# The first sub-layer's opening by quarters instead of halves, with joined shift and scale steps and fewer condition products on TensorE

## The chip, the core and the metric

The kernel runs on one core of a Trainium2 chip. TensorE multiplies, VectorE, ScalarE and GpSimd do element-wise work, SyncE issues most DMAs. The metric is the device time of one execution in microseconds; before, it is 1519.99 us (median of 3 runs, 1519.05 to 1521.19).

## What is computed

Two layers, each a half-step SwiGLU network, a hybrid token mixer and a second half-step SwiGLU network, on 256 tokens of 1024 features in float32. The change touches only what stands ahead of the first network: the normalised input is scaled and shifted by two rows that come from the condition vector c through the matrix w_ada.

```python
mod = jax.nn.silu(c) @ w_ada[i] + b_ada[i]
sh1, sc1, g1, sh2, sc2, g2, sh3, sc3, g3 = jnp.split(mod, 3 * N_SUBLAYERS, axis=-1)
h = modulate(rms_norm(x, norm_pre[i, 0]), sh1, sc1)      # h * (1 + scale) + shift
y = swiglu_ffn(h, w_ffn_in[i, 0], w_ffn_out[i, 0])
x = x + 0.5 * g1[:, None, :] * rms_norm(y, norm_post[i, 0])
```

## The kernel before

There are six sub-layers (s = 0 to 5). Each streams its weights in chunks of 512 KB. SyncE loads a chunk into one of eight `w_raw` slots, ScalarE rounds it into `w_hi` (line 1213), VectorE computes the remainder `w_lo` = `w_raw` - `w_hi` (line 1522), and TensorE multiplies. For each weight tile it makes three products: `w_hi` with `h_hi` (717), `w_lo` with `h_hi` (718), `w_hi` with `h_lo` (710). A chunk of the first network's input matrix is twelve such products of 512 columns. Each engine runs its own list in program order; semaphores join the lists, and an instruction that waits holds up all behind it on its engine.

A chunk of the input matrix is a pair (u, q): unit u (0 to 10) is 512 output columns (256 gate, 256 up), q (0 to 3) is one quarter of the 1024 rows, so it needs one quarter of the features of h. Sub-layer 0 takes its chunks in `FIRST_ORDER`: units 0 to 2 with q = 0 and 1 (chunks 0 to 5), then units 0 to 2 with q = 2 and 3 (chunks 6 to 11), then unit by unit. When a unit has its four chunks, ScalarE takes silu of the gate part, VectorE multiplies (`act_by_token`, 1722), TensorE turns the result (`act_turn`, 752); chunk 12 is the first of unit 3, ahead of which `act_turn(1)` stands.

To have h at all, sub-layer 0 needs the scale row (part 1 of `ada_acc`) and the shift row (part 0), each the sum of 8 slabs of w_ada (128 rows each, times one element of silu(c) per partition) and a bias, and then a sum over the 128 partitions. One slab step on VectorE is a `scalar_tensor_tensor` that adds slab times c to the accumulator (`first_steps`, 1550); each waits for the step before it. The first half (512 features) of the scale row is made wholly on TensorE (862, 866), two of eight slabs of the shift's first half too (883); the other 22 half-steps run on VectorE. Then VectorE scales x by the row (1561, 1571), TensorE multiplies by the diagonal of the root mean square (`rstd_diagonal`) which also turns the tile (894), and adds the shift in the same bank (901); ScalarE rounds to `h_hi` (1285), VectorE takes `h_lo` (1581). This is done in two halves: the second stands between chunks 3 and 5 on TensorE.

Of the kernel before, what the change touches and what calls it, by code (L numbers as in the profile page):

```python
# [11 lines left out]
ALU = mybir.AluOpType  # L12
AX_X = mybir.AxisListType.X

P = 128
# [59 lines left out]
FIRST_ORDER = [(u, q) for u in range(EARLY) for q in (0, 1)] + [(u, q) for u in range(EARLY) for q in (2, 3)]  # L75
# [192 lines left out]
def build(nc, x_d, c_d, w_ada, b_ada, norm_pre, norm_post, w_ffn_in, w_ffn_out, w_in, pool_w, w_ret_out, w_pool_out,  # L268
          w_ssm_out, w_fox_out, w_out, vecs_d, consts_d, out_d):
    with ExitStack() as ctx:  # L270
# [49 lines left out]
        DG, dg_off = sb("rstd_diagonal", [P, TT, P])  # L320
# [104 lines left out]
        first_a_ps = sem("first_half_scale_row_in_psum")  # L425
        first_pre = [sem(f"first_pre_row_landed{s}") for s in range(2)]
        late_x = sem("second_half_x_scaled")
# [128 lines left out]
        def _(sp):  # L556
# [50 lines left out]
            def pre_row(t):  # L607
                if t == 1:
                    sp.wait_ge(late_x, 2)
# [12 lines left out]
            def first_slabs(n, half, pair):  # L622

                ks = slice(2 * pair * P, (2 * pair + 2) * P)
                col = PARTS[n] * D + half * HALF
                sp.dma_start(PSLAB[:, 8 * n + 2 * pair:8 * n + 2 * pair + 2, half * HALF:(half + 1) * HALF],
                             w_ada[0, ks, col:col + HALF].rearrange("(k p) n -> p k n", p=P))\
                    .then_inc(ada_first[8 * n + 4 * half + pair], 16)
# [8 lines left out]
            first_slabs(0, 0, 0)  # L637
            for order, n in enumerate(PARTS):
                bias(0, n, order)
            for pair in range(1, 4):  # L640
                first_slabs(0, 0, pair)
            sp.dma_start(KC[:, 0:P], consts_d[:, 0:P]).then_inc(ident_landed, 16)
            first_row(0)
            for pair in range(4):
                first_slabs(1, 0, pair)
            for g in range(3):
                chunk(g)
            first_slabs(0, 1, 0)
            first_slabs(0, 1, 1)
            chunk(3)  # L650
            first_slabs(0, 1, 2)
            first_slabs(0, 1, 3)
            first_row(1)
            first_slabs(1, 1, 0)
            first_slabs(1, 1, 1)
            chunk(4)
            first_slabs(1, 1, 2)
            first_slabs(1, 1, 3)
            for g in range(5, N_RAW):
                chunk(g)  # L660
# [3 lines left out]
            for s in range(SUBS):  # L664
                l = s // 3
                for c in range(COUNT[s]):
# [3 lines left out]
                    if s + 1 < SUBS and c == 3:  # L670
# [21 lines left out]
        def _(pe):  # L692
# [10 lines left out]
            def token_chunk(g, j, banks, hi, lo, kn, tts, lo_ready=None):  # L703

                wh, wl = weights(g)
                parts = [(kk, tt) for kk in range(2) for tt in tts]
# [20 lines left out]
            def ffn_in(s, c):  # L727
# [7 lines left out]
                if s == 0 and c == 0:  # L735
                    pe.wait_ge(hh_ok.sem, hh_ok.at(0, 2))

                    def ready():
                        pe.wait_ge(hl_ok.sem, hl_ok.at(0, 2))
                if s == 0 and c == 2 * EARLY:  # L740
                    pe.wait_ge(hl_ok.sem, hl_ok.at(0, 4))
# [117 lines left out]
            def first_scale_row():  # L859

                pe.wait_ge(bias_landed[1].sem, bias_landed[1].at(0, 16))
                mm(PS[:, 4, :], ones, part(1)[:, 0:HALF], start=True, stop=False)
                for k in range(KD):
                    if k % 2 == 0:
                        pe.wait_ge(ada_first[k // 2], 16)
                    ins = mm(PS[:, 4, :], CS[:, k:k + 1].to_broadcast([P, P]), PSLAB[:, k, 0:HALF], start=False,  # L866
                             stop=(k == KD - 1))
                ins.then_inc(first_a_ps, 1)

            def late_scale_row():  # L870

                pe.wait_ge(first_used, FIRST_SCALE)
                pe.wait_ge(hl_ok.sem, hl_ok.at(0, 2))
                mm(PS[:, 6, :], ones, part(1)[:, HALF:D], start=True, stop=True).then_inc(a_ps.sem, 1)

            def first_pair_of_shifts():

                pe.wait_ge(ada_first[8], 16)
                pe.wait_ge(xsq_ok.sem, xsq_ok.at(0, 4))
                for tt in range(TT):  # L880
                    for k in range(4):
                        for i in range(2):
                            mm(PS[:, 6 + tt, k * P:(k + 1) * P], PSLAB[:, 8 + i, k * P:(k + 1) * P],
                               CS[:, i:i + 1].to_broadcast([P, P]), start=(k == 0 and i == 0), stop=False)

            def first_turn(half, tt):

                if half == 0:
                    pe.wait_ge(f_ok.sem, scaled(0, tt + 1))
                else:  # L890
                    pe.wait_ge(late_x, tt + 1)
                for k in range(4):
                    cs = slice(half * HALF + k * P, half * HALF + (k + 1) * P)
                    mm(PS[:, 6 + tt, k * P:(k + 1) * P], Y[:, tt, cs], DG[:, tt, :], start=(half == 1 and k == 0), stop=False)

            def first_shifts(half, tt):

                pe.wait_ge(first_used, FIRST_SHIFT if half == 0 else LATE_SHIFT)
                for k in range(4):
                    cs = slice(half * HALF + k * P, half * HALF + (k + 1) * P)  # L900
                    ins = mm(PS[:, 6 + tt, k * P:(k + 1) * P], part(0)[:, cs], ones, start=False, stop=(k == 3))
                ins.then_inc(t_ps.sem, 1)
# [10 lines left out]
            def ffn(s):  # L913
# [272 lines left out]
            first_scale_row()  # L1186
            first_pair_of_shifts()
            for tt in range(TT):
                first_turn(0, tt)
            for tt in range(TT):  # L1190
                first_shifts(0, tt)
# [8 lines left out]
        def _(act):  # L1200
# [80 lines left out]
            def first_h_hi(half):  # L1281

                for tt in range(TT):
                    act.wait_ge(t_ps.sem, t_ps.at(0, 2 * half + tt + 1))
                    fn(HH[:, 4 * half:4 * half + 4, tt * P:(tt + 1) * P], PS[:, 6 + tt, :].rearrange("p (k t) -> p k t", k=4),
                       ACT.Copy).then_inc(hh_ok.sem, 1)
# [35 lines left out]
            def ffn(s):  # L1322
                f = 2 * (s // 3) + (s % 3) // 2
                for c in range(N_FFN - TAIL):
# [13 lines left out]
                    if s == 0 and c == 1:  # L1338
                        split_to(6)
                        first_h_hi(1)  # L1340
# [14 lines left out]
            def mixer(s):  # L1355
                layer = s // 3
                n_gate, n_sz, n_xbc = 0, 0, 0
                for c in range(N_MIX - TAIL):
# [62 lines left out]
                    if c == 1 and layer == 0:  # L1421
                        fn(SEL[0:32, :], ident[0:32, 0:20], ACT.Copy)
                        fn(SEL[32:64, :], ident[32:64, 32:52], ACT.Copy)
# [74 lines left out]
            split_to(0)  # L1498
            first_h_hi(0)
            split_to(4)  # L1500
# [8 lines left out]
        def _(dve):  # L1509
# [31 lines left out]
            def first_steps(a, b):  # L1541

                for m in range(a, b):
                    n, half, k = FIRST_STEPS[m]
                    cs = slice(half * HALF, (half + 1) * HALF)
                    dve.wait_ge(ada_first[8 * n + 4 * half + k // 2], 16)
                    dve.wait_ge(bias_landed[PARTS[n]].sem, bias_landed[PARTS[n]].at(0, 16))
                    if m:
                        dve.wait_ge(first_used, m)
                    dve.scalar_tensor_tensor(part(PARTS[n])[:, cs], PSLAB[:, 8 * n + k, cs], CS[:, k:k + 1],  # L1550
                                             part(PARTS[n])[:, cs], ALU.mult, ALU.add).then_inc(first_used, 1)

# [624 lines left out]
```

## Time and profile before

| | before |
|---|---|
| median of 3 runs | 1519.99 us |
| profiled execution, its time | 1519.76 us |
| profiled execution, its span | 1517.7 us |
| TensorE busy | 1487.8 us, 98% |
| VectorE busy | 1134.8 us, 75% |
| ScalarE busy | 778.9 us, 51% |
| DMA, mean over the span | 226 GB/s |

The span runs from the first to the last instruction that the profile holds; the time of the same execution is 2.1 us more. TensorE is busy nearly all the time, so the question for an edit at the start is when it gets into that state, and how much of its work is done by then.

### The profile page before, as it was taken

To read this page: it belongs to the slowest core of one execution; us is meant where nothing else is said; L and a number is where in the kernel's file an instruction comes from. 1 tells how busy PE (TensorE), PEld (TensorE's weight loads), DVE (VectorE), ACT (ScalarE), POOL (GpSimd) and SP (SyncE) were. 2 spreads that over 40 slices of the span, in tenths; PEclk is the share of its full clock that TensorE was granted. 3 is DMA by queue.
4 is the path that set the end of the run, shared out by engine and by line. 5 is a ranking of instruction groups with operands and counts; after the bars stand their busy time and mean duration, and the time that the engine had idled before them with its cause. 6 is when DMAs were issued, how large, how long until landed. Compare 5 with 4: busy or idle time off the path is not lost.

```text
span 1517.7 us, 20003 instructions
## 1 busy us (share of the span) xinstructions
PE 1487.8 (98%) x7776; PEld 1260.4 (83%) x7776; DVE 1134.8 (75%) x1339; ACT 778.9 (51%) x970; POOL 165.5 (11%) x96
## 2 busy tenths in 40 slices
PE   7999999999999999999999999999999999999998
PEld 4788888998978887888878888799988888878886
DVE  5887767867899888677686777767878988774453
ACT  3444455556473556454464444654746545654443
POOL 0000002303411110000000000040324011000000
PEclk9999999999999999999999999999999999999999
DMA  9899866656677856888768887565567787556652
GB/s 355 285 305 298 310 217 210 174 151 190 201 245 248 276 182 221 258 275 274 239 200 258 279 268 252 174 192 158 167 199 230 239 266 243 175 181 185 187 188 97
DMA packets 199778, 343.42 MB, mean 226 GB/s; under 512 B 18546, under 2 KB 109938, under 8 KB 199684
## 3 DMA queue, kind: packets, MB, share of 16 engines
q1 hardware_dynamic: 181540, 276.08, 57.9%
q10 hardware_dynamic: 18144, 66.07, 13.1%
q8 instruction: 61, 1.00, 0.3%
q14 instruction: 33, 0.27, 0.1%
HBM read 341.05 MB, written 1.05 MB: 225 GB/s over the span
## 4 chain that ended last, share of the span: by engine, by line
PE 87%; DVE 9%; issue 2%; ACT 2%; DMA 0%; SPq 0%; ACTq 0%; DVEq 0%
PE ps L717 16%; PE ps L710 16%; PE ps L718 16%; PE ps L794 6%; PE ps L795 6%; PE ps L796 6%; PE ps L1151 4%; PE ps L1153 4%; PE ps L1152 4%; DVE w_lo L1522 2%; DVE ada_acc L1538 1%; PE ps L752 1%; DVE ada_acc L1550 1%; PE ps L835 1%; PE ps L866 1%
## 5 line engine op out<-in xcount | busy, mean ns | idle before, releaser
L1522 DVE TENSOR_TENSOR w_lo<-w_raw,w_hi 128x1024 fp32r<-128x1024 f32 x480 | 611.4, 1296 | 110.6 <-ACT w_hi L1213 110.2
L1213 ACT ACTIVATE w_hi<-w_raw 128x1024 fp32r<-128x1024 f32 x490 | 507.6, 1053 | 353.7 <-DMA w_raw<-in_w_ffn_in 121.2
L717 PE MATMUL ps<-w_hi,h_hi 128*128 128x512 f32 x1026 | 407.4, 397 | 4.6 <-DVE w_lo L1522 3.1
L718 PE MATMUL ps<-w_lo,h_hi 128*128 128x512 f32 x1026 | 400.5, 390 | 0.0
L710 PE MATMUL ps<-w_hi,h_lo 128*128 128x512 f32 x1026 | 398.0, 391 | 0.0
L717 PEld LDWEIGHTS ps<-w_hi,h_hi 128*128 128x128 f32 x1026 | 193.0, 188 | 47.9 <-DVE w_lo L1522 6.5
L710 PEld LDWEIGHTS ps<-w_hi,h_lo 128*128 128x128 f32 x1026 | 192.7, 188 | 42.2 <-DVE h_lo L1678 1.0
L718 PEld LDWEIGHTS ps<-w_lo,h_hi 128*128 128x128 f32 x1026 | 193.3, 188 | 38.3
L1538 DVE SCALAR_TENSOR_TENSOR ada_acc<-ada_slab,c_silu,ada_acc 128x1024 f32<-128x1024 f32 x128 | 187.0, 1461 | 14.1 <-DMA ada_slab<-in_w_ada 14.1
L1151 PE MATMUL ps<-h_hi,w_hi 128*128 128x256 f32 x640 | 183.0, 286 | 0.0
L1153 PE MATMUL ps<-h_hi,w_lo 128*128 128x256 f32 x640 | 181.0, 283 | 0.0
L1152 PE MATMUL ps<-h_lo,w_hi 128*128 128x256 f32 x640 | 181.0, 283 | 0.0
L794 PE MATMUL ps<-w_hi,act_hi 128*128 128x512 f32 x352 | 137.6, 391 | 0.0
L795 PE MATMUL ps<-w_lo,act_hi 128*128 128x512 f32 x352 | 137.0, 389 | 0.0
L796 PE MATMUL ps<-w_hi,act_lo 128*128 128x512 f32 x352 | 137.0, 389 | 0.0
L1722 DVE TENSOR_TENSOR act_by_token<-gate_silu,ps 128x512 f32<-128x512 f32 x44 | 30.2, 687 | 131.5 <-PE ps L710 118.0
L1151 PEld LDWEIGHTS ps<-h_hi,w_hi 128*128 128x128 f32 x640 | 122.7, 192 | 1.2 <-issue 0.3
L1152 PEld LDWEIGHTS ps<-h_lo,w_hi 128*128 128x128 f32 x640 | 122.8, 192 | 0.2
L1153 PEld LDWEIGHTS ps<-h_hi,w_lo 128*128 128x128 f32 x640 | 122.7, 192 | 0.0
L2038 POOL MEMSET ada_acc<- 128x1024 f32 x18 | 17.0, 953 | 644.6 <-PE ps L847 597.5
L1333 ACT ACTIVATE gate_silu<-ps 128x512 f32<-128x512 f32 x44 | 26.3, 597 | 111.9 <-PE ps L710 111.3
L796 PEld LDWEIGHTS ps<-w_hi,act_lo 128*128 128x128 f32 x352 | 66.1, 188 | 13.9
(286 smaller groups left out, 1666.8 us busy)
## 6 DMA issues: line engine op xcount, KB each, us to landing
w_raw<-in_w_ffn_in SPq DMA_DIRECT2D x352, 256.0 KB, 3.6
w_raw<-in_w_in SPq DMA_DIRECT2D x168, 512.0 KB, 3.7
ada_slab<-in_w_ada ACTq DMA_DIRECT2D x126, 512.0 KB, 4.7
w_raw<-in_w_ffn_out SPq DMA_DIRECT2D x88, 512.0 KB, 4.4
ada_slab_first<-in_w_ada SPq DMA_DIRECT2D x16, 512.0 KB, 8.8
w_raw<-in_w_ssm_out SPq DMA_DIRECT2D x16, 512.0 KB, 4.4
w_raw<-in_w_out SPq DMA_DIRECT2D x16, 512.0 KB, 3.4
w_raw<-in_w_pool_out SPq DMA_DIRECT2D x8, 512.0 KB, 3.7
```

The source lines that it names most:

```text
L710: return mm(PS[:, banks + tt, :], lo[:, k, tok(tt)], wh[:, kk * HALF:(kk + 1) * HALF], start=False, stop=(k == kn - 1))
L717: mm(out, hi[:, k, tok(tt)], wh[:, cs], start=(k == 0), stop=False)
L718: mm(out, hi[:, k, tok(tt)], wl[:, cs], start=False, stop=False)
L794: mm(out, hi[:, k, tok(tt)], wh[:, cs], start=first, stop=False)
L795: mm(out, hi[:, k, tok(tt)], wl[:, cs], start=False, stop=False)
L796: return mm(out, lo[:, k, tok(tt)], wh[:, cs], start=False, stop=last)
L1151: mm(out, wh[:, cs], HH[:, k, :], start=(k == 0 and t % 2 == 0), stop=False)
L1152: mm(out, wh[:, cs], HL[:, k, :], start=False, stop=False)
L1153: ins = mm(out, wl[:, cs], HH[:, k, :], start=False, stop=(k == KD - 1 and t % 2 == 1))
L1213: fn(WH[:, n % N_HI, 0:width], RAW[:, n % N_RAW, 0:width], ACT.Copy).then_inc(w_hi, 1)
L1522: dve.tensor_tensor(WL[:, n % N_RAW, 0:width], RAW[:, n % N_RAW, 0:width], WH[:, n % N_HI, 0:width], ALU.subtract).then_inc(w_lo, 1)
L1538: dve.scalar_tensor_tensor(part(n), slab, CS[:, k:k + 1], part(n), ALU.mult, ALU.add)\
```

## The change

Chunks 0 to 11 are taken quarter by quarter: units 0 to 2 with q = 0, then 1, 2, 3. The slabs are loaded by quarters (256 columns, four slabs of one part per DMA, still 16 DMAs of 512 KB). One VectorE step now takes a slab's quarter of the shift and of the scale together (128 x 2 x 256). For the first quarter four of the eight slabs (0, 1, 4, 5) are products on TensorE, both parts in one product; for the other quarters all eight are VectorE steps. TensorE's product with ones sums both rows at once, once a quarter. The diagonal is gone: VectorE applies the root and the shift itself (`first_h_full`), and TensorE turns the result (`pe.transpose`, 4 per quarter). Other edits: for the first chunk of every quarter the products with `h_hi` and `w_hi` come first, then those with `w_lo`, then those with `h_lo`; ScalarE's silu table is loaded ahead of the first chunk; and the second sub-layer's row of norm_pre is asked for later.

```diff
-FIRST_ORDER = [(u, q) for u in range(EARLY) for q in (0, 1)] + [(u, q) for u in range(EARLY) for q in (2, 3)]
+QUARTER = D // 4
+FIRST_ORDER = [(u, q) for q in range(4) for u in range(EARLY)]
 FIRST_ORDER += [(u, q) for u in range(EARLY, UNITS) for q in range(4)]
...
-FIRST_STEPS = [(1, 0, k) for k in range(2, 8)] + [(0, 1, k) for k in range(8)] + [(1, 1, k) for k in range(ADA_FIRST)]
-FIRST_SHIFT, FIRST_SCALE, LATE_SHIFT = 6, 14, 22
+def on_pe(q):
+
+    return () if q else (0, 1, 4, 5)
+
+
+FIRST_STEPS = [(q, k) for q in range(4) for k in range(8) if k not in on_pe(q)]
...
+            def first_rows_of(q):
+
+                out = PS[:, 7, :].rearrange("p (n c) -> p n c", n=2)
+                slabs = PSLAB[:].rearrange("p (n k) c -> p n k c", n=2)
+                for i, k in enumerate(on_pe(q)):
+                    for n in range(2):
+                        pe.wait_ge(ada_first[4 * q + 2 * n + k // 4], 16)
+                    mm(out, CS[:, k:k + 1].to_broadcast([P, P]), slabs[:, :, k, q * QUARTER:(q + 1) * QUARTER], start=(i == 0),
+                       stop=False)
+                pe.wait_ge(first_used, first_steps_of(q)[1])
+                mm(out, ones, ACC[:, 0:2 * D].rearrange("p (n c) -> p n c", n=2)[:, :, q * QUARTER:(q + 1) * QUARTER],
+                   start=(not on_pe(q)), stop=True).then_inc(first_rows if q < 3 else a_ps.sem, 1)
+
+            def first_turn(q):
+
                 for tt in range(TT):
...
+                    for k in range(2):
+                        ins = pe.transpose(PS[:, 6, k * T + tt * P:k * T + (tt + 1) * P],
+                                           Y[:, tt, (2 * q + k) * P:(2 * q + k + 1) * P], ident)
                 ins.then_inc(t_ps.sem, 1)
...
-                    if s == 0 and c == 3:
-                        late_scale_row()
-                    if s == 0 and c in (4, 5):
-                        for tt in range(TT):
-                            (first_turn if c == 4 else first_shifts)(1, tt)
+                    if s == 0 and c in (2, 5, 8):
+                        first_rows_of(c // 3 + 1)
+                    if s == 0 and c in (3, 6, 9):
+                        first_turn(c // 3)
...
+            fn(DUMMY[:], one, ACT.Silu)
+            for q in range(4):
+                split_to(3 * q)
+                first_h_hi(q)
...
+            for q in range(4):
+                split_to(3 * q)
+                first_h_lo(q)
+                if q == 3:
+                    break
+                split_to(3 * q + 1)
+                first_steps(q + 1)
+                split_to(3 * q + 2)
...
+                first_x_scale(q + 1)
+                first_h_full(q + 1)
```

VectorE, from the first `h_lo` to the x scaling of the second half, before; `first_steps` is line 1550 and `split_to` line 1522:

```order
L1581 TENSOR_TENSOR h_lo<-ps,h_hi 128x4x128 x2
L1522 TENSOR_TENSOR w_lo<-w_raw,w_hi 128x1024
L1550 SCALAR_TENSOR_TENSOR ada_acc<-ada_slab_first,c_silu,ada_acc 128x512 x4
L1522 TENSOR_TENSOR w_lo<-w_raw,w_hi 128x1024
L1550 SCALAR_TENSOR_TENSOR ada_acc<-ada_slab_first,c_silu,ada_acc 128x512 x4
L1522 TENSOR_TENSOR w_lo<-w_raw,w_hi 128x1024
L1561 SCALAR_TENSOR_TENSOR scale_row<-ps,scale_row 128x512
L1571 TENSOR_TENSOR y_tok<-x_res,scale_row 128x512 x2
```

Now, from one quarter's `h_lo` (1576) to the next quarter's, with the steps in line 1545, the remainders in line 1512, the x scaling in 1563 and the root and shift in 1570; this block stands three times in a row:

```order
L1576 TENSOR_TENSOR h_lo<-ps,h_hi 128x512
L1512 TENSOR_TENSOR w_lo<-w_raw,w_hi 128x1024
L1545 SCALAR_TENSOR_TENSOR ada_acc<-ada_slab_first,c_silu,ada_acc 128x2x256 x8
L1512 TENSOR_TENSOR w_lo<-w_raw,w_hi 128x1024
L1556 SCALAR_TENSOR_TENSOR scale_row<-ps,scale_row 128x256
L1563 TENSOR_TENSOR y_tok<-x_res,scale_row 128x256 x2
L1570 SCALAR_TENSOR_TENSOR y_tok<-y_tok,small_columns,ps 128x256 x2
L1512 TENSOR_TENSOR w_lo<-w_raw,w_hi 128x1024
```

Eight steps in a row now stand ahead of each row sum, and three chunks' remainders are spread between them.

VectorE at the end of the opening, before, from the last `h_lo` (1581) to the product of the first finished unit (1722; 1538 is a slab step of the gate row):

```order
L1581 TENSOR_TENSOR h_lo<-ps,h_hi 128x4x128 x2
L1522 TENSOR_TENSOR w_lo<-w_raw,w_hi 128x1024 x6
L1722 TENSOR_TENSOR act_by_token<-gate_silu,ps 128x512
L1522 TENSOR_TENSOR w_lo<-w_raw,w_hi 128x1024
L1538 SCALAR_TENSOR_TENSOR ada_acc<-ada_slab,c_silu,ada_acc 128x1024
```

And now (1712 is that product, 1528 that slab step):

```order
L1576 TENSOR_TENSOR h_lo<-ps,h_hi 128x512
L1512 TENSOR_TENSOR w_lo<-w_raw,w_hi 128x1024 x3
L1528 SCALAR_TENSOR_TENSOR ada_acc<-ada_slab,c_silu,ada_acc 128x1024
L1512 TENSOR_TENSOR w_lo<-w_raw,w_hi 128x1024
L1528 SCALAR_TENSOR_TENSOR ada_acc<-ada_slab,c_silu,ada_acc 128x1024
L1712 TENSOR_TENSOR act_by_token<-gate_silu,ps 128x512
```

The first finished unit's product moved behind two slab steps; the last `h_lo` comes before chunk 9 and not before chunk 6.

## Rows read from the trace of the kernel before

**Rows 1.** Page, part 1: busy us, share of the span, instructions.
```profile
PE 1487.8 (98%) x7776; PEld 1260.4 (83%) x7776; DVE 1134.8 (75%) x1339; ACT 778.9 (51%) x970; POOL 165.5 (11%) x96
```

**Rows 2.** Stretches: busy time of each engine, PEclk (granted clock), DMA share, GB/s.
```profile
10.00:50.00 40.00, 35.02 (x167) 25.00 (x166) 29.14 (x42) 8.86 (x12) 0.95 (x1) 1.00 1.06 388
...
50.00:200.00 150.00, 150.00 (x687) 123.93 (x687) 119.87 (x115) 73.73 (x84) 3.81 (x4) 1.00 0.88 293
```

**Rows 3.** Waits of TensorE from 50 us on: us in total, times, longest.
```profile
PE ps L835 <- DVE y_tok L1669: 7.9, 5, 1.6
```

**Rows 4.** Chain of waits, 0 to 52 us, shares by line.
```profile
by line: DVE ada_acc L1550 28.9%; PE ps L866 16.5%; issue 12.2%; DMA ada_acc<-in_b_ada 10.4%; PE ps L901 7.9%; PE ps L862 3.9%; DVE y_tok L1571 2.7%; DVE scale_row L1561 2.7%; PE ps L874 2.2%; SPq L636 1.9%; ACT w_hi L1213 1.8%; DVEq L1549 
```

**Rows 5.** Timeline of VectorE: start us, us, what, idle before.
```profile
17.22 1.65 DVE L1550 SCALAR_TENSOR_TENSOR ada_acc<-ada_slab_first,c_silu,ada_acc 128x512 f32<-128x512 f32 x2 [5.90 <-DMA ada_slab_first<-in_w_ada]
...
34.12 3.40 DVE L1550 SCALAR_TENSOR_TENSOR ada_acc<-ada_slab_first,c_silu,ada_acc 128x512 f32<-128x512 f32 x4
...
37.44 1.22 DVE L1522 TENSOR_TENSOR w_lo<-w_raw,w_hi 128x1024 fp32r<-128x1024 f32 x1
...
39.22 0.69 DVE L1561 SCALAR_TENSOR_TENSOR scale_row<-ps,scale_row 128x512 f32<-128x512 f32 x1 [0.57 <-PE ps L874]
...
50.89 0.69 DVE L1581 TENSOR_TENSOR h_lo<-ps,h_hi 128x512 fp32r<-128x512 f32 x1 [0.51 <-ACT h_hi L1285]
...
52.39 6.89 DVE L1522 TENSOR_TENSOR w_lo<-w_raw,w_hi 128x1024 fp32r<-128x1024 f32 x6
...
61.95 1.28 DVE L1538 SCALAR_TENSOR_TENSOR ada_acc<-ada_slab,c_silu,ada_acc 128x1024 f32<-128x1024 f32 x1
```

**Rows 6.** Groups of VectorE by form, whole span: count, busy us, mean ns.
```profile
L1550 DVE SCALAR_TENSOR_TENSOR ada_acc<-ada_slab_first,c_silu,ada_acc 128x512 f32<-128x512 f32 x22 | 16.5, 750 | 8.0 <-DMA ada_slab_first<-in_w_ada 5.9
...
L1911 DVE SCALAR_TENSOR_TENSOR xbc<-xbc,vectors,ps 128x256 f32<-128x256 f32 x16 | 6.9, 471 | 0.0
```

**Rows 7.** Timeline of TensorE's products.
```profile
10.17 8.79 PE L866 MATMUL ps<-ada_slab_first,c_silu 128*128 128x512 f32 x16
...
27.60 0.50 PE L717 MATMUL ps<-w_hi,h_hi 128*128 128x512 f32 x1 [0.69 <-ACT h_hi L1285]
...
37.58 1.12 PE L874 MATMUL ps<-ada_acc,small_columns 128*128 128x512 f32 x2 [0.29 <-DVE ada_acc L1550]
...
45.75 0.50 PE L717 MATMUL ps<-w_hi,h_hi 128*128 128x512 f32 x1 [2.22 <-DVE w_lo L1522]
...
67.95 0.60 PE L752 MATMUL ps<-consts,act_by_token 128*128 128x128 f32 x4
...
68.31 0.48 PE L717 MATMUL ps<-w_hi,h_hi 128*128 128x512 f32 x1
...
71.16 0.39 PE L717 MATMUL ps<-w_hi,h_hi 128*128 128x512 f32 x1
```

**Rows 8.** Timeline of TensorE's weight loads.
```profile
8.30 0.50 PEld L862 LDWEIGHTS ps<-ada_acc,small_columns 128*128 128x128 f32 x2 [8.30 <-issue]
...
12.74 0.34 PEld L866 LDWEIGHTS ps<-ada_slab_first,c_silu 128*128 128x128 f32 x1 [0.52 <-issue]
...
14.08 0.19 PEld L866 LDWEIGHTS ps<-ada_slab_first,c_silu 128*128 128x128 f32 x1 [0.24 <-issue]
```

**Rows 9.** Timeline of ScalarE.
```profile
26.95 0.60 ACT L1285 ACTIVATE h_hi<-ps 128x512 fp32r<-128x512 f32 x1 [0.30 <-PE ps L901]
...
27.44 2.95 ACT L1213 ACTIVATE w_hi<-w_raw 128x1024 fp32r<-128x1024 f32 x3
```

**Rows 10.** Timeline of SyncE's queue: the first slabs.
```profile
2.32 0.43 SPq L626 DMA_DIRECT2D ada_slab_first<-in_w_ada  x1
...
3.96 1.48 SPq L626 DMA_DIRECT2D ada_slab_first<-in_w_ada  x3
```

**Rows 11.** DMA issues, 2.3 to 2.7 us: KB, us to landing.
```profile
ada_slab_first<-in_w_ada SPq DMA_DIRECT2D x1, 512.0 KB, 5.7
```

**Rows 12.** DMA issues, 4.9 to 5.3 us: KB, us to landing.
```profile
ada_slab_first<-in_w_ada SPq DMA_DIRECT2D x1, 512.0 KB, 7.4
```

More of the change, by code:

```diff
@@ L243, in __call__, with first_steps_of @@
         self.need(self.mark(ins))
-FIRST_STEPS = [(1, 0, k) for k in range(2, 8)] + [(0, 1, k) for k in range(8)] + [(1, 1, k) for k in range(ADA_FIRST)]
-FIRST_SHIFT, FIRST_SCALE, LATE_SHIFT = 6, 14, 22
+def on_pe(q):
+    return () if q else (0, 1, 4, 5)
+FIRST_STEPS = [(q, k) for q in range(4) for k in range(8) if k not in on_pe(q)]
+def first_steps_of(q):
+    m = [i for i, step in enumerate(FIRST_STEPS) if step[0] == q]
+    return m[0], m[-1] + 1
 def vector_table(b_forget, pool_scale, conv_w, conv_b, dt_bias, a_log, d_skip, ssm_norm):
@@ L636, in _ @@
                 sp.dma_start(X[:, tt, :], x_d[0, tt * P:(tt + 1) * P, :]).then_inc(x_landed[tt], 16)
-            first_slabs(0, 0, 0)
+            first_slabs(0, 0)
             for order, n in enumerate(PARTS):
                 bias(0, n, order)
-            for pair in range(1, 4):
-                first_slabs(0, 0, pair)
+            first_slabs(0, 1)
+            first_row(0)
             sp.dma_start(KC[:, 0:P], consts_d[:, 0:P]).then_inc(ident_landed, 16)
[L643 to L659, printed above, removed]
+            for q in range(4):
+                if q:
+                    first_slabs(q, 0)
+                    first_slabs(q, 1)
+                    if q == 2:
+                        first_row(1)
+                chunk(2 * q)
+                chunk(2 * q + 1)
+            for g in range(8, N_RAW):
                 chunk(g)
@@ L669, in _ @@
                     chunk(BASE[s] + c + N_RAW)
-                    if s + 1 < SUBS and c == 3:
+                    if s + 1 < SUBS and c == (3 if s else 10):
                         pre_row(s + 1)
@@ L703, in token_chunk @@
             def token_chunk(g, j, banks, hi, lo, kn, tts, lo_ready=None):
+                parts = [(kk, tt) for kk in range(2) for tt in tts]
+                if g < 3 * EARLY + 1 and lo_ready is not None:
+                    pe.wait_ge(w_hi, g + 1)
+                    wh = WH[:, g % N_HI, :]
+                    for kk, tt in parts:
+                        mm(PS[:, banks + tt, :], hi[:, 2 * j + kk, tok(tt)], wh[:, kk * HALF:(kk + 1) * HALF],
+                           start=(2 * j + kk == 0), stop=False)
+                    _, wl = weights(g)
+                    for kk, tt in parts:
+                        mm(PS[:, banks + tt, :], hi[:, 2 * j + kk, tok(tt)], wl[:, kk * HALF:(kk + 1) * HALF], start=False,
+                           stop=False)
+                    lo_ready()
+                    for kk, tt in parts:
+                        k = 2 * j + kk
+                        ins = mm(PS[:, banks + tt, :], lo[:, k, tok(tt)], wh[:, kk * HALF:(kk + 1) * HALF], start=False,
+                                 stop=(k == kn - 1))
+                    return ins
                 wh, wl = weights(g)
-                parts = [(kk, tt) for kk in range(2) for tt in tts]
                 def lo_product(kk, tt):
@@ L857, in shift_sums @@
                 column_sums(0, t, bank).then_inc(sh_ps.sem, 1)
[L859 to L879, printed above, removed]
-                for tt in range(TT):
[L881 to L901, printed above, removed]
+            def first_rows_of(q):
+                out = PS[:, 7, :].rearrange("p (n c) -> p n c", n=2)
+                slabs = PSLAB[:].rearrange("p (n k) c -> p n k c", n=2)
+                for i, k in enumerate(on_pe(q)):
+                    for n in range(2):
+                        pe.wait_ge(ada_first[4 * q + 2 * n + k // 4], 16)
+                    mm(out, CS[:, k:k + 1].to_broadcast([P, P]), slabs[:, :, k, q * QUARTER:(q + 1) * QUARTER], start=(i == 0),
+                       stop=False)
+                pe.wait_ge(first_used, first_steps_of(q)[1])
+                mm(out, ones, ACC[:, 0:2 * D].rearrange("p (n c) -> p n c", n=2)[:, :, q * QUARTER:(q + 1) * QUARTER],
+                   start=(not on_pe(q)), stop=True).then_inc(first_rows if q < 3 else a_ps.sem, 1)
@@ L1185, in _ @@
             pe.wait_ge(c_ok, 1)
[L1186 to L1191, printed above, removed]
+            first_rows_of(0)
+            pe.wait_ge(xsq_ok.sem, xsq_ok.at(0, 4))
+            pe.wait_ge(ident_landed, 16)
+            first_turn(0)
             for s in range(SUBS):
@@ L1279, in h_hi, with first_h_hi @@
                        PS[:, 2 * tt + half, :].rearrange("p (k t) -> p k t", k=4), ACT.Copy).then_inc(hh_ok.sem, 1)
[L1281 to L1286, printed above, removed]
+            def first_h_hi(q):
+                act.wait_ge(t_ps.sem, t_ps.at(0, q + 1))
+                fn(HH[:, 2 * q:2 * q + 2, :], PS[:, 6, :].rearrange("p (k t) -> p k t", k=2), ACT.Copy).then_inc(hh_ok.sem, 1)
             def boundary(s):
```

129 lines of the change are left out of this document (55 added, 74 removed).

## The prediction, made before the changed kernel ran

> **What bounds the kernel now.** I read the page first: TensorE is busy 98% of the span [rows 1], so an edit pays or costs only through the time at which TensorE gets its work. The stretches say where that is open: from 50 to 200 us TensorE is busy in all of 150 us, from 10 to 50 us in 35.0 of 40, and much of that is not network work but the making of the rows [rows 2]. After 50 us the largest wait is 7.9 us at the five later boundaries, which the change leaves alone [rows 3]. So the whole effect is this: at what time does TensorE start chunk 12 (by then chunks 0 to 11 and two `act_turn` are done in both kernels)? Before, that is 71.16 us [rows 7]. What is behind it is paced by TensorE.
>
> Inside the opening the chain of waits puts 28.9% on VectorE's slab steps, more than on any other line, and 16.5% on the first rows' products on TensorE [rows 4]. The timeline of VectorE shows the steps in packs of four, a remainder `w_lo` between them, with no idle time ahead of the packs [rows 5]; TensorE waits for VectorE ahead of chunk 4 for 2.22 us [rows 7]. The DMA share is full (1.06, 388 GB/s) [rows 2], but VectorE waits for a slab once only, ahead of the first pack [rows 5]. So VectorE paces the opening once the first slabs are in.
>
> **Unit costs.** A pack of four steps takes 3.40 and one is 0.75 long, so a dependent step comes every (3.40 - 0.75) / 3 = 0.88 us [rows 5, 6]. `w_lo` is 1.22 long, six take 6.89, one each 1.13 [rows 5]. The gate row's step is 1.28, about 1.20 apart [rows 5]. ScalarE rounds a chunk in 1.06 (three in 2.95) and an `h_hi` tile in 0.60, 0.50 apart [rows 9]. A row sum on TensorE is 1.12 [rows 7]; a turn of four tiles lands in 0.60 and holds TensorE for 0.36 (67.95 to 68.31) [rows 7]; chunk 11 takes 2.85 (68.31 to 71.16), of which the turn's tail is about 0.1, so a chunk alone is 2.72 to 2.75 [rows 7]; I use 2.72 and 0.1 behind a turn. The joined step (128 x 2 x 256) is in no row. The nearest is the 512-column step, same elements, 0.75; from below it is bounded by 0.47, the 256-column form of the operation, from above by two of those, 0.94 [rows 6]. With the 0.13 of the wait: 0.60 to 1.07, and I take 0.88, since both ends would need cost to go by rows and not by elements. The 256-column scaling and shifting operations: 0.47 each [rows 6], five in 2.1 with their overlaps.
>
> **The first quarter.** The first slab lands at 2.3 + 5.7 = 8.0, the fourth at 4.95 + 7.4 = 12.35 (its issue is the third one's of the three from 3.96) [rows 10 to 12]; at 388 GB/s the second is 1.35 behind the first, 9.4. Here four slab DMAs are the whole quarter. VectorE: two steps from 9.5, two from 12.4, end 14.05, then the five small operations of the second root to 15.2. TensorE: products at 9.4 and 11.1 at the slow pace (weight loads 0.34 long, 0.52 between, 1.7 per product; 0.19 and 0.24 later, 0.86 per product [rows 8]), then two more with the quicker pace coming in between, then the sum: 16.5, with 15.7 if the quick pace comes at once at 12.8, and 17.4 if only at the end. Then 2.1 for VectorE's five (18.7), the turn and `h_hi` (19.8). Chunks 0 and 1 are 0.33 MB (row and identity) and 1.05 MB behind the fourth slab, 3.6 us at 388 GB/s, so in by 16, ahead of their use. TensorE starts chunk 0 at 19.8 where it did at 27.60 [rows 7]: 7.8 us earlier. Behind `h_hi` ScalarE rounds chunk 1 (20.8), VectorE takes its remainder, and the second quarter's first step starts at 21.95.
>
> **The cycle of a quarter.** From there, in order: eight steps 7 x 0.88 + 0.75 = 6.9; the remainder of chunk 3q+2, 1.22 (TensorE's row sum, 1.12, lies beside it at no cost; without that cover it would add 1.1); 0.1 for semaphores; chunk 3q+2 on TensorE, 2.72, because `first_turn` stands behind it; the turn 0.6; `h_hi` 0.50 until ScalarE is free; then ScalarE's rounding of chunk 3q+4, 1.06, which stands behind `h_hi`, and its remainder on VectorE, 1.13; 0.1. Sum 14.4. VectorE's scaling and shift (2.1), one remainder and `h_lo` lie beside chunk 3q+2 and the turn: work of 2.1 + 1.2 against 3.3, so they cost nothing, but also hide nothing more. Data isn't late: the slabs of the second quarter are 3.5 MB behind the first quarter's last, 9 us at 388 GB/s, so 21.4, just ahead of the first step, and a later quarter needs 3.7 MB in 14.4 us. Over three cycles, `h_hi` of the fourth quarter starts at 21.95 + 2 x 14.4 + 11.7 = 62.4 (11.7 is the cycle up to there).
>
> **The end of the opening.** Chunk 9 starts at 63.1, chunk 10 ends at 68.5. But chunk 11 stands behind `act_turn(0)`, and VectorE reaches that unit's product only after: rounding of chunk 10 on ScalarE (64.0), three remainders 3.4, step 1.2, remainder 1.13, step 1.2, product 0.7: 71.65. TensorE waits 3.2 us there, turns, chunk 11 from 72.1, turn, chunk 12 at 75.1. Against 71.16 that is 3.9 us later. The balance in another way: VectorE does 28 steps instead of 22 (6 x 0.88 = 5.3 us more), and none of TensorE's freed time can be used.
>
> **The sum.** 1519.76 (profiled execution) + 3.9 = 1523.7. The median of the runs is 0.2 above that execution, so 1523.9; I say 1524.0. A difference under 0.2%, 3.0 us, can't be told from none.
>
> **A rival by the clock of TensorE.** The granted clock reads 1.00 in all stretches [rows 2], and yet the same weight load takes 0.34 early and 0.19 from 14 us [rows 8], as if between 1.2 and 2.4 GHz, after TensorE had been busy for 5 us. The new opening has TensorE idle three times for 3.4 us (chunk 3q+1 ends 3.4 ahead of the row sum), and 3.2 before `act_turn(0)`. The longest pause before was 2.22, and the product behind it took the usual 0.50, as at 27.60 [rows 7]; no row shows a longer one here. If the pace falls, a row sum costs 1.8 instead of 1.1 and chunk 3q+2 up to 1.6 more; both are in the cycle: 2 us each quarter, 6 us in all, 1530.
>
> The Trainium skill ("TensorE: Matmul & The Clock Gate", Part 1, the HAM clock gate) says that an idle TensorE falls back to 1.2 GHz, which speaks against this change; by that rule the sum would be the 1530 of this rival, by the row of the 2.22 us pause 1524.
>
> **Other rivals.** The joined step is cheap: if it goes at the pace of its 256-element rows, 0.60, each quarter is 2 us shorter: 3.9 - 6.0, 1518; it needs 0.55 or less to win over 0.2%. For it: the opening's chain is these steps. Against it: 22 rows of the 512-column form at 0.75, and 0.47 for half of that, a cost by elements [rows 6]. This is the case on the other side. A plainer form of it, that the 7.8 us gained at chunk 0 simply stay, would give 1512; it needs VectorE's cycle to be TensorE's (three chunks, sum, turn: 9.7 us), and the eight steps alone are 6.9 of that with three remainders behind them; I give it nothing of its own.
>
> The loss is real but small: the quick pace comes early (15.7, -0.8) and semaphores and the idle tenths that I add come to less; 1520 to 1523, not to be told from no change. For it: my terms hold 0.1 to 0.3 us per quarter of such waits.
>
> **Chances.** Forecast mechanism with over 3.0 us lost: 0.58. Clock falls: 0.10. Same mechanism but under 3.0 us, 0.22, and a step somewhat cheaper, 0.03. Cheap step that wins: 0.07. So faster 0.07, same 0.25, slower 0.68. The likeliest case alone spans 1523 to 1526 (first rows at 15.7 to 17.4, waits). The range has to reach the clock's 1530 above and the small loss below: 1519.5 to 1530.
>
> **What would show it.** Right: first product of chunk 0 near 19.8; joined steps 0.75 long; first steps of the quarters 14.4 apart; TensorE idle about 3.4 us ahead of each row sum and about 3 us ahead of the first `act_turn`; chunk 12 at 75. Wrong: joined steps near 0.5 or 0.9, VectorE idle on slabs, products of chunk 2, 5, 8 at twice their length, or TensorE busy throughout from 45 us on.

## The result and the profile after

The changed kernel takes 1531.93 us (median of 4 runs, 1529.38 to 1533.34), the kernel before 1520.59 us on the same chip (4 runs, 1519.05 to 1522.37). The ratio is 1.0071, with a 95% interval of 1.0059 to 1.0084: slower by 0.7%, or 11.3 us. The forecast was 1524.0 with a range up to 1530, so the sign was right and the loss nearly three times as large as said. The profiled execution took 1531.35 us with a span of 1529.5.

First the page of after, its part 1 (busy time, share of the span, instructions), which answers to [rows 1]:

```profile
PE 1485.6 (97%) x7692; PEld 1255.1 (82%) x7692; DVE 1143.8 (75%) x1357; ACT 778.5 (51%) x971; POOL 165.5 (11%) x96
```

TensorE has 84 products fewer and 2.2 us less of busy time, and the span is 11.8 us longer. So the time is not lost with more work; it goes to TensorE being idle, or to the same products taking longer. The stretches of after tell where (columns as in [rows 2]: busy time of PE, PEld, DVE, ACT, POOL, then the granted clock, DMA share, GB/s):

```profile
20.00:40.00 20.00, 15.41 (x59) 11.43 (x60) 16.07 (x23) 6.10 (x7) 0.00 (x0) 0.91 1.09 383
40.00:60.00 20.00, 13.78 (x51) 9.75 (x49) 15.70 (x22) 4.50 (x5) 0.00 (x0) 0.91 0.82 287
60.00:82.00 22.00, 17.33 (x58) 12.93 (x59) 17.63 (x21) 8.43 (x10) 1.90 (x2) 0.77 0.48 160
82.00:200.00 118.00, 118.00 (x540) 97.52 (x539) 97.09 (x93) 57.24 (x65) 2.87 (x3) 1.00 0.90 299
```

TensorE is idle for 4.6, 6.2 and 4.7 us in the three stretches from 20 us on, and the granted clock, 1.00 in both rows of [rows 2], is 0.91, 0.91 and 0.77. From 82 to 200 us it is never idle and the clock reads 1.00. The DMA share is full up to 40 us and falls after that, and none of the waits below is for a DMA.

The waits of TensorE from 19 to 83 us (us in total, times, longest) name what it waits for; the two largest:

```profile
PE ps L885 <- DVE ada_acc L1545: 10.0, 3, 3.3
PE ps L768 <- DVE act_by_token L1712: 2.9, 1, 2.9
```

The last joined step of a quarter holds up the row sum (885) three times for 3.3 us, and the first unit's product (1712) holds up `act_turn` (768) once for 2.9. The chain of events is plainest in TensorE's timeline of after, which answers to [rows 7] (start, us, what, idle before):

```profile
9.55 6.73 PE L882 MATMUL ps<-ada_slab_first,c_silu 128*128 128x512 f32 x8 [9.55 <-DMA ada_slab_first<-in_w_ada]
...
20.59 1.20 PE L712 MATMUL ps<-w_hi,h_hi 128*128 128x512 f32 x4 [0.69 <-ACT h_hi L1277]
...
29.65 2.08 PE L885 MATMUL ps<-ada_acc,small_columns 128*128 128x512 f32 x2 [3.31 <-DVE ada_acc L1545]
30.79 1.37 PE L735 MATMUL ps<-w_hi,h_hi 128*128 128x512 f32 x1
31.95 0.63 PE L736 MATMUL ps<-w_lo,h_hi 128*128 128x512 f32 x1
...
34.85 0.60 PE L896 MATMUL ps<-consts,y_tok 128*128 128x128 f32 x4
36.13 1.19 PE L712 MATMUL ps<-w_hi,h_hi 128*128 128x512 f32 x4 [0.69 <-ACT h_hi L1277]
...
45.19 1.12 PE L885 MATMUL ps<-ada_acc,small_columns 128*128 128x512 f32 x2 [3.32 <-DVE ada_acc L1545]
46.33 0.72 PE L735 MATMUL ps<-w_hi,h_hi 128*128 128x512 f32 x1
...
50.08 0.39 PE L735 MATMUL ps<-w_hi,h_hi 128*128 128x512 f32 x1
...
50.77 0.60 PE L896 MATMUL ps<-consts,y_tok 128*128 128x128 f32 x4
52.06 1.19 PE L712 MATMUL ps<-w_hi,h_hi 128*128 128x512 f32 x4 [0.69 <-ACT h_hi L1277]
...
61.12 2.07 PE L885 MATMUL ps<-ada_acc,small_columns 128*128 128x512 f32 x2 [3.32 <-DVE ada_acc L1545]
62.25 1.37 PE L735 MATMUL ps<-w_hi,h_hi 128*128 128x512 f32 x1
...
67.56 0.60 PE L896 MATMUL ps<-consts,y_tok 128*128 128x128 f32 x4
68.85 1.20 PE L712 MATMUL ps<-w_hi,h_hi 128*128 128x512 f32 x4 [0.69 <-ACT h_hi L1277]
...
77.45 1.12 PE L768 MATMUL ps<-consts,act_by_token 128*128 128x128 f32 x4 [2.87 <-DVE act_by_token L1712]
78.22 0.78 PE L735 MATMUL ps<-w_hi,h_hi 128*128 128x512 f32 x1
...
82.15 0.60 PE L768 MATMUL ps<-consts,act_by_token 128*128 128x128 f32 x4
82.50 0.48 PE L735 MATMUL ps<-w_hi,h_hi 128*128 128x512 f32 x1
```

Chunk 0 starts at 20.59, 7.0 us earlier than before, and chunk 12 at 82.50, 11.3 later than the 71.16 of [rows 7]. That is nearly the whole loss: 1529.5 - 82.50 = 1447.0 us behind it, against 1517.7 - 71.16 = 1446.5 before. And behind each of these four pauses products are longer: 0.63, one every 0.43, instead of 0.39, one every 0.23. In chunk 5 they are short again from 50.08 on. The granted clock falls with them, to half (a stretch inside chunk 5, columns as above):

```profile
46.50:49.80 3.30, 3.30 (x8) 2.56 (x9) 3.12 (x6) 0.00 (x0) 0.00 (x0) 0.50 1.10 387
```

Chunk 2 takes 30.79 to 34.85, 4.06; chunk 5 46.33 to 50.77, 4.44; chunk 8 62.25 to 67.56, 5.31; the turn and chunk 11 77.45 to 82.15, 4.70. Without slow products a chunk behind a row sum takes 2.86, and the turn with chunk 11 takes 3.25 (both measured in the first experiment below). The excess is 1.20 + 1.58 + 2.45 + 1.45 = 6.7 us. The other 11.3 - 6.7 = 4.6 is what the forecast put at 3.9; chunk 0 alone starts 0.8 later than its forecast.

VectorE does what was reckoned. Its timeline of after (columns as above) has the pack of joined steps in it:

```profile
22.66 6.93 DVE L1545 SCALAR_TENSOR_TENSOR ada_acc<-ada_slab_first,c_silu,ada_acc 128x512 f32<-128x512 f32 x8
```

(6.93 - 0.75) / 7 = 0.88 from one to the next, as before [rows 5, 6].

### The profile page after: what moved, and what is told of

Its sections match the earlier page's. It is cut to its first block, busy times and chain, and to the rows that moved or that the text cites. A ratio compares the mean times of both kernels' runs of the same rounds, so it can differ in the third digit from the quotient of the medians.

```text
span 1529.5 us, 19867 instructions
## 1 busy us (share of the span) xinstructions
PE 1485.6 (97%) x7692; PEld 1255.1 (82%) x7692; DVE 1143.8 (75%) x1357; ACT 778.5 (51%) x971; POOL 165.5 (11%) x96
## 4 chain that ended last, share of the span: by engine, by line
PE 85%; DVE 9%; issue 2%; ACT 2%; DMA 1%; SPq 0%; DVEq 0%; ACTq 0%
PE ps L735 16%; PE ps L728 16%; PE ps L736 16%; PE ps L810 6%; PE ps L811 6%; PE ps L812 6%; PE ps L1146 4%; PE ps L1148 4%; PE ps L1147 4%; DVE w_lo L1512 2%; DVE ada_acc L1528 1%; PE ps L768 1%; DVE ada_acc L1545 1%; ACT w_hi L1206 1%; PE ps L1022 1%
## 5 line engine op out<-in xcount | busy, mean ns | idle before, releaser
L736 PE MATMUL ps<-w_lo,h_hi 128*128 128x512 f32 x1010 | 396.4, 392 | 0.0
L812 PEld LDWEIGHTS ps<-w_hi,act_lo 128*128 128x128 f32 x352 | 66.1, 188 | 13.9
```

Of the source, the lines that this page charges most:

```text
L736: mm(out, hi[:, k, tok(tt)], wl[:, cs], start=False, stop=False)
L812: return mm(out, lo[:, k, tok(tt)], wh[:, cs], start=False, stop=last)
```

## The experiments

Theory A: the loss is the forecast's longer VectorE path (3.9 us) and, on top, a slower TensorE behind each long pause (about 7 us). Theory B: the slow products have another cause (contention, the new product shapes, the place in the program), and what is lost is just the wait for VectorE. All ratios are against the kernel before, run on the same chip, with 95% intervals.

**1. The same waits with TensorE kept busy (e1_warm).** Unused products in bank 7 fill the pauses; everything else is as in after. They read tiles that have long been in place; 14 stand ahead of each later row sum and 12 ahead of the first `act_turn`.

```
+            def keep_busy(n):
+                for _ in range(n):
+                    mm(PS[:, 7, :], HH[:, 0, tok(0)], HH[:, 0:2, :], start=True, stop=True)
...
+                    if s == 0 and c == 11:
+                        keep_busy(12)
...
                     if s == 0 and c in (2, 5, 8):
+                        keep_busy(14)
                         first_rows_of(c // 3 + 1)
```

> The changed kernel with idle-time work: fourteen products of 512 columns on tiles that are in place anyway (results unused) ahead of each of the three later row sums, and twelve ahead of the first finished unit's turn, so that TensorE has no pause over 2 us there. Nothing else differs. Theory A (the slab steps on VectorE lengthen the quarter's cycle by what I worked out, and the rest of the loss is TensorE's pace, which falls in the pauses of 3.3 us): no product of chunks 2, 5, 8 and 11 longer than 0.5 us, chunk 12 at 75.5, time 7 us under the changed kernel, 1525. Theory B (the pace isn't lost through the pauses but through something else in the new order, as the quarter's data or the row sum itself): slow products remain, 1532. Theory C (the loss is VectorE's alone, the slow products being hidden): products normal, but time within 2 us of 1532.

Measured: 1524.00 us (10 runs, 1522.91 to 1526.88), ratio 1.0024 (1.0015 to 1.0033); 7.9 us less than after by the medians, 7.4 by the spans of the two profiled executions (1522.1 and 1529.5), with 54 products more. TensorE's timeline of this kernel around the second row sum, at the first `act_turn` and at the start of chunk 12:

```profile
40.10 3.33 PE L891 MATMUL ps<-h_hi 128*128 128x512 f32 x14
43.59 1.12 PE L885 MATMUL ps<-ada_acc,small_columns 128*128 128x512 f32 x2 [0.16 <-DVE ada_acc L1553]
44.73 0.50 PE L735 MATMUL ps<-w_hi,h_hi 128*128 128x512 f32 x1
...
47.59 0.60 PE L901 MATMUL ps<-consts,y_tok 128*128 128x128 f32 x4
...
71.82 0.66 PE L768 MATMUL ps<-consts,act_by_token 128*128 128x128 f32 x4
...
75.43 0.48 PE L735 MATMUL ps<-w_hi,h_hi 128*128 128x512 f32 x1
```

The row sum still comes when VectorE lets it, but the chunk behind it takes 2.86 instead of 4.44. The stretch of this kernel from 40 to 60 us reads 1.00 where after reads 0.91:

```profile
40.00:60.00 20.00, 18.98 (x78) 13.62 (x77) 17.10 (x25) 4.50 (x5) 0.88 (x1) 1.00 0.86 306
```

Theory A holds: without the idle time of TensorE no product of the opening is slow, though the order, the shapes and the transfers are those of after. Chunk 12 starts at 75.43, 7.1 us earlier than in after: 6.7 for the slow products and 0.4 because chunk 0 starts at 20.15 in this execution. Against before it is 4.3 us late, where the forecast said 3.9.

**2. and 3. TensorE takes part of the slabs again (e2_two_pe, e3_four_pe).** Two of eight products and six steps in each later quarter, or four and four.

```
 def on_pe(q):
-    return () if q else (0, 1, 4, 5)
+    return (0, 4) if q else (0, 1, 4, 5)
```

That is with two; with four the line is `return (0, 1, 4, 5)`.

> The changed kernel with slabs 0 and 4 of the second to fourth quarter made on TensorE and six steps instead of eight on VectorE. Theory A: a quarter's cycle on VectorE is two steps (1.8 us) shorter, the two products (0.86 each) fill the pause, so the pace doesn't fall: quarters 12.6 us apart, chunk 12 at 70.5 to 72, 1519.5 to 1521. Theory C (VectorE's steps alone): 3 x 1.8 = 5.3 us less than the changed kernel, 1526.5. Theory D (the order by quarters, shared by both forms, costs the loss): 1530 or more.

> As the run with two slabs on TensorE, but four (0, 1, 4, 5) in every quarter. Theory A: VectorE's cycle would be 10.9 us, but TensorE's becomes the longer: four products 3.4, sum 1.1, three chunks 8.2, turn 0.4, pause for h_hi 0.9, 14.0 us; pace stays high; chunk 12 at 72 to 73, 1521 to 1522. Theory C: another 5.3 us less than with two, 1521 at the lower end. A rival by which products on TensorE are free in its pauses: 1517.

Measured: with two 1520.75 us (1518.75 to 1523.58), ratio 1.0002 (0.9992 to 1.0011); with four 1523.14 (1522.05 to 1524.73), ratio 1.0019 (1.0009 to 1.0029). With two, this is inside the expected 1519.5 to 1521; with four it is 1.1 us over the expected 1521 to 1522, whose reckoning had the quarter's cycle right (14.0) but no pause ahead of `act_turn`. In neither is there a pause ahead of a row sum. The quarters start 13.8, 12.7 and 12.6 us apart with two, 13.9 with four: there VectorE waits up to 3.5 us for the row sum behind TensorE's four slab products. Both keep a pause of 2.9 ahead of `act_turn`; with two, slow products follow it, with four none do.

With two, chunk 0 is slow as well: it takes 4.46 instead of the 2.87 of after, behind the pause of 2.02 ahead of the first turn that all kernels with the change have, and that is why the first of the three distances is the longest. TensorE's timeline with two:

```profile
19.35 1.49 PE L712 MATMUL ps<-w_hi,h_hi 128*128 128x512 f32 x4 [0.69 <-ACT h_hi L1277]
...
23.81 0.40 PE L735 MATMUL ps<-w_hi,h_hi 128*128 128x512 f32 x1
...
67.08 0.66 PE L768 MATMUL ps<-consts,act_by_token 128*128 128x128 f32 x4 [2.87 <-DVE act_by_token L1712]
67.50 0.48 PE L735 MATMUL ps<-w_hi,h_hi 128*128 128x512 f32 x1
...
71.91 0.60 PE L768 MATMUL ps<-consts,act_by_token 128*128 128x128 f32 x4
```

Chunk 11 takes 4.41 here, 2.85 with four. So of the whole change the part that costs is that the later quarters' slabs all went to VectorE. The opening by quarters with joined steps and two of eight slabs on TensorE comes out even with before.

**4. The gate row's steps later (e4_gate_late).** In after, two of them stand ahead of the first unit's product on VectorE, and so cause the last pause.

```
-            places.setdefault(8 + int(1.4 * (i - ADA_FIRST)), []).append((0, i))
+            places.setdefault(12 + (i - ADA_FIRST), []).append((0, i))
```

> The changed kernel with the gate row's eight steps at chunks 12 to 19 instead of 8 to 17, so that no such step stands ahead of the first finished unit's product on VectorE. Theory A: TensorE's pause ahead of that turn (2.87 us) shrinks to 0.5 or less and the slow products of chunk 11 go with it: 4.5 us under the changed kernel, 1527.5; the three earlier falls of the pace remain. Rival (the steps only move the wait to chunks 12 to 19): within 1.5 us of 1532.

Measured: 1530.24 us (1528.59 to 1531.28), ratio 1.0061 (1.0046 to 1.0076): 1.7 less than after, where 4.5 was expected. TensorE's timeline of this kernel shows the pause gone, but not the gain:

```profile
75.22 0.66 PE L768 MATMUL ps<-consts,act_by_token 128*128 128x128 f32 x4 [0.44 <-DVE act_by_token L1712]
...
105.33 0.66 PE L768 MATMUL ps<-consts,act_by_token 128*128 128x128 f32 x4 [0.76 <-DVE act_by_token L1712]
...
1337.78 1.32 PE L851 MATMUL ps<-consts,y_tok 128*128 128x128 f32 x8 [1.56 <-DVE y_tok L1659]
...
1340.17 0.63 PE L736 MATMUL ps<-w_lo,h_hi 128*128 128x512 f32 x1
```

Chunk 12 starts at 78.8, 3.7 earlier. Of that, 0.8 is waited for at 105 us, because the steps were only moved; and this execution has slow products from 1340 to 1343 us, behind a later boundary's pause, where after's has none (the same instructions take 1.6 us longer than in after). 3.7 - 0.8 - 1.6 = 1.3, against 1.5 between the two spans. The 1.6 belongs to this execution: the slow pieces differ from profile to profile, which is also why a single profile says less than a median here. Why the medians, with four runs of each, lie only 1.7 apart too stays open.

**5. to 7. Shorter pauses (e5_warm_half, e6_warm_three, e10_warm_half_timed).** 7 or 3 unused products instead of 14 ahead of each row sum, none ahead of `act_turn`; the last is the same kernel as the first, timed.

```
                     if s == 0 and c in (2, 5, 8):
+                        keep_busy(7)
                         first_rows_of(c // 3 + 1)
```

> The changed kernel with seven unused products instead of fourteen ahead of each of the three later row sums, and none ahead of the turn of chunk 11: the three pauses become 1.7 us, the fourth stays 2.9. Theory A (the pace falls in a long pause only): chunks 2, 5 and 8 at the usual 0.23 us per product, chunk 11 can be slow for some products as before; quarters 14.4 us apart; 1524 to 1526. Rival (any pause of VectorE's making slows the next products): slow products stay.

> As the run with seven, but three unused products: pauses of 2.6 us. Before had one of 2.2 us without slow products behind it, the changed kernel ones of 3.3 with slow products behind all. Theory A: between these two; if 2.6 is harmless, 1524 to 1526 and no slow product in chunks 2, 5 and 8; if it is harmful now and then, some chunks are slow and the time is 1526 to 1530.

> The same kernel as the run with seven unused products, timed. In its one profile the pace fell behind one of three pauses of 1.7 us and behind the one of 2.9. Theory A (pauses of this length lower the pace sometimes): median between the full filling's 1524.0 and the changed kernel's 1531.9, at 1526 to 1527.5, and a spread over 3 us. Rival (that fall was an exception): 1525 or less.

Measured: one run each, 1526.9 with 7 products (expected 1524 to 1526) and 1526.87 with 3 (inside the 1526 to 1530 expected if a pause of 2.6 is harmful now and then); timed with 7: 1525.36 (1524.45 to 1527.14), ratio 1.0032 (1.0021 to 1.0043). That is under the 1526 to 1527.5 expected, and the spread is 2.7 where over 3 was expected; it is above the rival's 1525 or less. TensorE's timeline with 7 products (e5_warm_half): two pauses of the same length, one harmless, one not.

```profile
43.63 1.12 PE L885 MATMUL ps<-ada_acc,small_columns 128*128 128x512 f32 x2 [1.73 <-DVE ada_acc L1551]
44.76 0.50 PE L735 MATMUL ps<-w_hi,h_hi 128*128 128x512 f32 x1
...
57.97 1.12 PE L885 MATMUL ps<-ada_acc,small_columns 128*128 128x512 f32 x2 [1.75 <-DVE ada_acc L1551]
59.11 0.74 PE L735 MATMUL ps<-w_hi,h_hi 128*128 128x512 f32 x1
```

In the timed kernel's profile the slow products stand behind another of these pauses, and in chunk 0. So pauses of 1.7 and of 2.9 us sometimes cost and sometimes don't, and with 3 products two of the three pauses of 2.6 did. The experiments changed the lengths only; what decides a single case they don't show.

**8. The old order with a longer pause (e8_before_pause).** Two useless VectorE operations in the kernel before lengthen its own pause ahead of chunk 4. If the new shapes or their place were the cause, no product would turn slow here.

```
             first_x_scale(1, 1)
+            for _ in range(2):
+                chain(dve.tensor_tensor(SHROW[:], X[:, 0, :], X[:, 1, :], ALU.mult))
             first_steps(FIRST_SCALE, 18)
```

> The kernel before the change with two useless VectorE operations of 1024 elements (1.2 us each, written to a buffer that nothing reads then) ahead of the steps for which chunk 4 waits. TensorE's pause ahead of chunk 4 grows from 2.2 to 4.6 us. Theory A (a long pause lowers TensorE's pace whatever the order of the work): products behind the pause take about 0.43 us from start to start instead of 0.23 for some microseconds; 2.4 us for the two operations and 1 to 2.5 us for the pace: 1524 to 1525.5. Rival (slow products belong to the new order alone): products at 0.23, 1523.

Measured: 1524.02 us (1522.97 to 1525.67), ratio 1.0024 (1.0015 to 1.0033). TensorE's timeline of this kernel at chunk 4, the place of [rows 7] with 2.22 of idle time:

```profile
47.62 0.79 PE L717 MATMUL ps<-w_hi,h_hi 128*128 128x512 f32 x1 [4.73 <-DVE w_lo L1522]
48.22 0.63 PE L718 MATMUL ps<-w_lo,h_hi 128*128 128x512 f32 x1
...
52.48 0.42 PE L710 MATMUL ps<-w_hi,h_lo 128*128 128x512 f32 x1
```

Chunk 4 starts 1.9 later, and its last product 4.86 behind its first, where it was 2.62. The granted clock reads 0.50 from 45.8 to 52.4 us. So the same happens in code without any of the change's edits.

**9. and 10. Both pauses taken away (e7_two_pe_gate_late, e9_two_pe_gate_ten).** Two products in each later quarter, and the gate row's steps either as late as in the fourth experiment or from chunk 10 on, one every 1.25 chunks.

```
-            places.setdefault(8 + int(1.4 * (i - ADA_FIRST)), []).append((0, i))
+            places.setdefault(10 + int(1.25 * (i - ADA_FIRST)), []).append((0, i))
...
-    return () if q else (0, 1, 4, 5)
+    return (0, 4) if q else (0, 1, 4, 5)
```

> Two slabs of eight on TensorE in the later quarters, and the gate row's eight steps at chunks 12 to 19. Theory A: the run with two slabs stood level with the kernel before and kept one pause of 2.9 us ahead of the first turn, with slow products behind it; late gate steps took 2.4 us of that pause away. So 2.4 us plus the slow products' 1.5 under the run with two slabs: 1516.8, 0.25% under before. Rival (the steps come back as waits at chunks 12 to 19): level with before.

> Two slabs of eight on TensorE, and the gate row's eight steps at chunks 10, 11, 12, 13, 15, 16, 17 and 18, each behind the product of the unit that ended there, and not packed into chunks 12 to 19. Theory A: with them at 12 to 19 chunk 12 started 3 us before the old kernel's, but TensorE waited 1.1 us for VectorE at chunks 17 and 21; spread, the wait goes while the first turn still has none: 3 us under before, 1517.3. Rival (any place this early delays the first unit's product or the later ones): level with before, 1519.5 or more.

Measured: with the steps at chunks 12 to 19 1519.57 us (1516.44 to 1522.42), ratio 0.9994 (0.9984 to 1.0003), 2.8 over the expected 1516.8: a miss. TensorE waits later on for 0.62 and 0.48 us (at 83.17 and 95.22), and slow products stand behind two of the five boundaries. The two runs whose mean granted clock is 1.000 took 1516.44 and 1516.52; the nine others, at 0.995 to 0.998, took 1518.42 to 1522.42. With the steps from chunk 10 on 1517.01 (1515.94 to 1519.11), ratio **0.9976** (0.9967 to 0.9986), with 1517.3 expected. It is the only version whose interval lies wholly under 1, by 0.24%. TensorE's timeline of it:

```profile
58.44 1.20 PE L712 MATMUL ps<-w_hi,h_hi 128*128 128x512 f32 x4 [0.69 <-ACT h_hi L1277]
...
64.66 0.66 PE L768 MATMUL ps<-consts,act_by_token 128*128 128x128 f32 x4 [0.48 <-DVE act_by_token L1712]
...
68.27 0.48 PE L735 MATMUL ps<-w_hi,h_hi 128*128 128x512 f32 x1
```

The fourth quarter starts at 58.44 and chunk 12 at 68.27, 2.9 us ahead of before. The span is 2.6 shorter. Against the version with steps at chunks 12 to 19 the span is 2.7 shorter: 1.1 are that version's two waits, and the other 1.6 is about what its second slow piece costs. So part of the difference between these two is which pauses happened to cost.

## Why the prediction was right in part, and the step that failed

**What bounds the kernel; where the effect sits.** Right. 11.3 of the 11.8 us between the spans is the start of chunk 12; the five later boundaries wait 8.0 us against 7.9 [rows 3].

**The joined step, 0.88.** Right to 0.01. The rival of a cheap step (0.60) falls with it: the joined step of two times 256 elements takes 0.75, as the one of 512 in a row does.

**The first quarter.** The first slab product came at 9.55 (9.4 forecast), chunk 0 at 20.59 (19.8): 0.8 late, since the row sum is done only at 17.1 and not at 16.5; what stands between it and chunk 0 takes the rest.

**The cycle, 14.4.** Right where TensorE is not slow: 14.38, 14.34 and 14.35 in the first experiment (the forecast's terms add up to 14.33). In after it is 15.5, 15.9 and 16.8, and 14.3 each when the excess of chunks 2, 5 and 8 is taken off. The pauses were forecast at 3.4 and 3.2 and are 3.3 and 2.9.

**The sum without the clock, 1524.0.** The first experiment, which is after without its idle time, measured 1524.00. That the two agree to the last digit is luck: chunk 12 stood at 75.43 and not at 75.1, and the kernel before measured 1520.62 beside it and not the 1519.99 that the forecast started from.

**The step that failed** is the clock rival, set at a chance of 0.10 on the words "The longest pause before was 2.22, and the product behind it took the usual 0.50 ... no row shows a longer one here". The sum itself priced a pause at its own length only. One harmless pause was taken as evidence for pauses of 3.3; the runs showed slow products behind all six pauses of 3.3 and behind three of six of 2.9, and 6.7 us of the loss is theirs. The rival's size was off too: "2 us each quarter, 6 us in all" was near for the quarters (1.20 + 1.58 + 2.45 = 5.2), but left out chunk 11 behind the pause at `act_turn` (1.45), which the forecast itself had put at 3.2 us. So even this rival stopped at 1530, short of the 1531.93 measured; with chunk 11 it would have given 1531.4.

The row that would have told it stood in the trace of before. The prediction set the 7.9 us of the boundaries aside as "which the change leaves alone" and read only what they cost in waiting. TensorE's timeline of before at the third boundary:

```profile
780.18 1.32 PE L835 MATMUL ps<-consts,y_tok 128*128 128x128 f32 x8 [1.56 <-DVE y_tok L1669]
781.64 0.71 PE L717 MATMUL ps<-w_hi,h_hi 128*128 128x512 f32 x1
782.14 0.63 PE L718 MATMUL ps<-w_lo,h_hi 128*128 128x512 f32 x1
...
785.13 0.40 PE L710 MATMUL ps<-w_hi,h_lo 128*128 128x512 f32 x1
```

and its stretch from 780 to 790 us:

```profile
780.00:790.00 10.00, 9.67 (x38) 7.63 (x39) 9.93 (x11) 5.14 (x8) 0.00 (x0) 0.83 0.45 151
```

A pause of 1.56 us, and behind it 3 us of products of 0.63, with a mean clock of 0.83 over these 10 us. The forecast's "reads 1.00 in all stretches [rows 2]" rests on two stretches that end at 200 us, ahead of the first of the five boundaries (232.94). And a long stretch blurs such a piece: from 700 to 800 us the column reads 0.98.

The Trainium skill ("TensorE: Matmul & The Clock Gate", Part 1, the HAM clock gate) says that an idle TensorE falls back to 1.2 GHz. The traces agree: the granted clock reads 0.50 among the slow products (46.5 to 49.8 us), and 0.43 per product against 0.23 is 1.9 times as long, near the ratio of 2.4 to 1.2 GHz.

## What to carry to other kernels

Here TensorE is the bound, and moving work from it to another engine gained nothing, since TensorE had no other work to put there. A pause that opens costs its own length and, in these profiles, often more in slow products behind it (1.1 to 2.7 us behind the pauses of 3.3), so price both, and do so for every pause, not only for those at the edit. Before calling a pause harmless, read stretches of 5 to 10 us and single products behind each pause that the kernel has already, since one harmless case is no rule. If a pause can't be avoided, unused products in it can bring the second part back (7.4 to 7.9 us here).

## What the runs showed of the chip

How long TensorE pauses does not by itself decide the pace behind the pause. In the twelve profiles of this case slow products follow

- 14 of the 60 pauses of 1.6 to 1.7 us at the boundaries, and 2 of 5 of 1.7 in the opening;
- 2 of 10 of 2.0 ahead of the first turn, and not the one of 2.2 in before;
- 2 of 3 of 2.6, 3 of 6 of 2.9, all 6 of 3.3 and the one of 4.7.

So the longest pauses always cost and shorter ones sometimes do, but the share does not rise evenly with the length. Every profile has one or two slow pieces at a boundary, now at one, now at another; each costs some 1.6 us at most (eight products, each 0.2 later). The spread of the runs goes with them: of the 62 runs of before that were timed beside the experiments, the one with a mean granted clock of 1.000 took 1518.12 us, the 27 at 0.998 took 1519.89 in the median and the 15 at 0.996 took 1521.02. No experiment steered the pieces, so this is shown as going together, not as the whole cause of the spread.

The length of the slow piece differs as well: behind equal pauses of 3.3 us, chunk 2 lost 1.20, chunk 5 1.58 and chunk 8 2.45. What sets it stays open.

The granted clock of before reads 1.00 from 10 to 50 us [rows 2], and in that stretch a weight load takes 0.34 at first and 0.19 later [rows 8]. At the start of this program the column doesn't show the slow pace; the lengths of equal instructions do.
